# Attention stage of a decoder layer: the last projection unit moved into eight steps of four rows, the newton steps and tile turns of two units respaced

## The chip, the core and the metric

One core of a Trainium2 chip runs the whole kernel. The metric is the device time in microseconds (us); the median of 3 runs of the kernel before is 889.22 us (888.16 to 891.59).

## The reference

```python
def reference(x, p, rel_bias, attn_norm, w_in, ...):
    for i in range(DEPTH):                      # DEPTH = 1, SEQ = 512, D_MODEL = 1024
        h = rms_norm(x, attn_norm[i])
        (mq, mk, mv, nsq, kc, vc, ksl, vsl, kwn, vwn, ngate, mgate) = jnp.split(h @ w_in[i], cuts, axis=-1)
        y_a = moba_attention(rms_norm(mq), rms_norm(mk), mv, tab_moba)          # 8 heads
        y_b = nsa_attention(rms_norm(nsq), kc, vc, ksl, vsl, kwn, vwn, ngate)   # 8 heads, 3 branches
        g_a, g_b = jnp.split(jax.nn.sigmoid(mgate), 2, axis=-1)
        x = x + (g_a * (y_a @ w_br_moba[i]) + g_b * (y_b @ w_br_nsa[i])) @ w_o[i]
        u = causal_dwconv(rms_norm(x, ffn_norm[i]) @ w_up[i], conv_w[i], conv_b[i])
        u_act, u_lin = jnp.split(u, 2, axis=-1)
        x = x + (jax.nn.gelu(u_act) * u_lin) @ w_down[i]
        x = x + jax.nn.sigmoid(x @ w_ple_gate[i]) * (p[i] @ w_ple[i])
    return x
```

The change touches nothing of what is computed. It concerns `h @ w_in`, and the norm over each head of its q and k columns, which are made while the attention of earlier heads runs.

## The kernel before

The kernel is written out by hand for five engines, each with its own instruction stream; semaphores join them. After a start stage comes the attention stage, a list of 100 steps (`STEPS`), and then the dense stages.

**Pairs and steps.** Heads are taken in eight pairs n. Pairs 0 to 3 are MoBA heads and have 8 steps each (two heads e, four query tiles i). Pairs 4 to 7 are NSA heads and have 17 steps each: 8 of the branch slc, 8 of win, and one of cmp. So pair 4 is steps 32 to 48, pair 5 steps 49 to 65, pair 6 steps 66 to 82, pair 7 steps 83 to 99. One step t goes through all engines: `scores(t)` on TensorE (L1629, L1630, or L1625 for cmp), `bias(t)` on VectorE (L1290, or L1298 to L1301 for cmp), `exp(t)` on ScalarE (L886, L883), `invert(t)` on VectorE, which its loop issues one step later behind `bias(t + 1)` (L1308, or L1313 to L1316 for cmp), `scale(t)` on GpSimd (L710, L713), `turn_probs(t)` on TensorE three steps later (L1650, or L1647 for cmp), `take_probs(t)` on ScalarE (L911, L909), and `values` on TensorE five steps later, once for two heads (L1672). `scores(t)` waits for `bias(t - 2)`. Every engine works its steps in order, so an engine that is late with one part of a step is late with all that its stream has behind it.

**Units of the projection.** Beside these steps TensorE works off `h @ w_in` in units w. A unit has 32 rows, one for each of four token tiles tt and eight slices kt of the contraction; a row is three matmuls (`three`, L1491 to L1493), since each float32 operand is held as a high and a low part. Units 5 and 7 have 384 columns, unit 6 has 256. `PROJ` says which rows of which unit stand in which step. Unit 6 serves pairs 5 and 7, unit 7 serves pair 6; the first steps of pair 6 (66 to 69) need unit 7's tiles.

**What a unit needs and sets off.** Its weights come by DMA while the unit before is split. `SPLIT` names the steps in which two slices are split: ScalarE makes both high parts (`w_high`, L843), VectorE the low part of the even slice (`w_low`, L1173), GpSimd that of the odd one (`split_unit`, L683). TensorE waits for both before the row. When a tile's 8 rows are done, ScalarE takes it out of PSUM one step later (`take_proj`, L838), squares it (L853), VectorE sums it (L1224), and for two tiles together makes a first guess of the reciprocal root (`GUESS`, L1148 to L1150). GpSimd refines it in three rounds of four small operations (`ROOT`, L723 to L729), VectorE normalises each tile (`TILE`, L1257), TensorE turns it (`TURN`, L1551), and ScalarE and VectorE store it one step later (L875, L1276). The next tile's turn waits for the one before to be stored, as they share one PSUM bank, and for its own `normalise`.

**Merge gates.** `GATE` places rows of 512 columns of another part of `w_in` (unit j of 8 rows) in the steps; j = 7 has one row in each of steps 41 to 46 and two in 47, j = 8 one in each of 50 to 55 and two in 56. Steps 48, 49 and 57 have none. Their weights are split at `GSPLIT` steps (40 and 48 here): L923 on ScalarE, L1189 on VectorE, L687 on GpSimd.

**Banks.** `proj_bank` puts every tile of units 6 and 7 into PSUM bank 0, so the first row of a tile waits until ScalarE has taken the tile before (`qkv_done`). Bank 7 is that of the gates.

**Order inside a step.** TensorE: scores, `turn_probs(t - 3)`, values, a gate's rows if a tile of the projection opens in this step, the rows of the projection, otherwise the gate's rows here, then the turn of a tile. ScalarE: the gate, `take_proj` and its squares, `take_probs`, the stored tile, `exp`, the gate's split, the weights' split. VectorE: bias, invert, sums, the stored tile, the weights' split, normalise, guess, the gate's split. GpSimd: scale(t - 1), the weights' split, values of the unit, root, the gate's split.

Before the change unit 6 is projected in steps 28 to 35 at four rows a step, its roots stand in steps 33 and 37 (all three rounds in one step), its normalised tiles in 35, 37, 39 and 41, and its turns each one step later. Unit 7 is split in steps 41 to 44, projected in steps 43 to 58 at two rows a step, its roots stand in steps 52 and 60, its tiles in 54, 56, 62 and 64, and its turns one step later.

Of the kernel before, what the change touches and what calls it, by code (L numbers as in the profile page):

```python
# [73 lines left out]
def layer(nc, A, out):  # L74
# [46 lines left out]
    for w in range(2, W_UNITS):  # L121
        b0 = first_t[w - 2]
        if w == 2:
            start, counts, row = b0, (4, 4), ROWS - KT
        elif w < 6:
            start, counts, row = b0 - 4, (5, 6, 5, 5, 6, 5), 0
        elif w == 6:
            start, counts, row = b0 - 4, (4,) * 8, 0
        else:
            start, counts, row = b0 - 6, (2,) * 16, 0  # L130
        for a, count in enumerate(counts):
            PROJ[start + a] = (w, row, row + count)
            row += count
        split0 = b0 - 8 if w == 7 else b0 - 7
        for a in range(KT // 2):
            SPLIT[split0 + a] = (w, range(2 * a, 2 * a + 2))
        VALUES[start + len(counts)] = w
        ends = [t for t in sorted(PROJ) if PROJ[t][0] == w for r in range(*PROJ[t][1:]) if r % KT == KT - 1]
        for half in range(2):
            t = ends[2 * half + 1] + 1 if w > 2 else b0 + 2 * half  # L140
            GUESS[t] = (w, half)
            late = 1 if half and w < 6 else 0
            if late:
                ROOT[t + 1], ROOT[t + 2] = (w, half, range(1)), (w, half, range(1, 3))
            else:
                ROOT[t + 1] = (w, half, range(3))
            if w >= 6:
                late += 1
            for a in range(2):
                TILE[t + 2 + late + 2 * a], TURN[t + 3 + late + 2 * a] = (w, 2 * half + a), (w, 2 * half + a)  # L150

    def segments(t):

# [58 lines left out]
    with ExitStack() as ctx:  # L212
# [186 lines left out]
        def proj_bank(w, tt):  # L399

            if w == 0:
                return (0, 1, 4, 5)[tt]
            if w in (3, 4, 5):
                return 7 * (tt % 2)
            return 6 if w <= 2 and tt % 2 and (w, tt) != (2, 3) else 0

        def column(w, x):
# [1080 lines left out]
        def _(pe):  # L1488
# [22 lines left out]
            def project(w, tt, kts=range(KT)):  # L1511

                c = ucols(w)
                if kts[0] == 0:
                    before = 4 * w + tt - (1 if w > 5 or (w, tt) in ((2, 3), (3, 0)) else 2)
                    if before >= 0:
                        pe.wait_ge(qkv_done, before + 1)
                    if w in (3, 4, 5) and tt == 1:
                        pe.wait_ge(gate_tanh, w)
                for kt in kts:  # L1520
                    wait_weights(pe, w, kt)
                    pe.wait_ge(hT_lo, kt + 1)
                    t_ = slice(P * tt, P * (tt + 1))
                    ins = three(PS[:, proj_bank(w, tt), 0:c], hTh[:, kt, t_], hTl[:, kt, t_], Wh[:, kt, 0:c], Wl[:, kt, 0:c], kt == 0, kt == KT - 1)
                    if tt == NT - 1 and kt < KT - 1:
                        ins.then_inc(w_used, 1)
                if kts[-1] == KT - 1:
                    ins.then_inc(proj_filled, 1)
# [25 lines left out]
            def gate(j, kts=range(KT)):  # L1554

                if kts[0] == 0:
# [4 lines left out]
                        pe.wait_ge(vc_done, 1)  # L1561
                    if j in (3, 4, 5):
                        pe.wait_ge(qkv_done, 4 * j + 4)
                for kt in kts:
                    if kt == 4:
                        pe.wait_ge(g_lo[1], j + 1)
                    ins = three(PS[:, 7, :], Gh[j % 2][:, kt, :], Gl[j % 2][:, kt, :], hTh[:, kt, :], hTl[:, kt, :], kt == 0, kt == KT - 1)
# [360 lines left out]
```

## Time and profile before

| | |
|---|---|
| median of 3 runs | 889.22 us |
| time of the profiled execution | 890.37 us |
| its span, first to last instruction | 888.5 us |
| PE busy | 863.6 us (97%) |
| DVE busy | 378.0 us (43%) |
| ACT busy | 405.8 us (46%) |
| POOL busy | 425.3 us (48%) |

All times below are in us from the start of the span of that one execution. PE is TensorE, DVE VectorE, ACT ScalarE, POOL GpSimd. A row of a timeline gives the start, the duration, the engine, the line of the kernel, the operation and what it writes and reads; behind it, in brackets, how long the engine stood idle before it and who ended the wait. Matmuls are pipelined, so they overlap in the rows, and the distance of two starts is the cost of one. The attention stage runs from about 85 to 364; its steps 32 to 48 from 205.7, steps 49 to 65 from 253.4, step 66 from 294.7.

### The profile page before, as it was taken

To read this page: it belongs to the slowest core of one execution; us is meant where nothing else is said; L and a number is where in the kernel's file an instruction comes from. 1 tells how busy PE (TensorE), PEld (TensorE's weight loads), DVE (VectorE), ACT (ScalarE), POOL (GpSimd) and SP (SyncE) were. 2 spreads that over 40 slices of the span, in tenths; PEclk is the share of its full clock that TensorE was granted. 3 is DMA by queue.
4 is the path that set the end of the run, shared out by engine and by line. 5 is a ranking of instruction groups with operands and counts; after the bars stand their busy time and mean duration, and the time that the engine had idled before them with its cause. 6 is when DMAs were issued, how large, how long until landed. Compare 5 with 4: busy or idle time off the path is not lost.

```text
span 888.5 us, 13023 instructions
## 1 busy us (share of the span) xinstructions
PE 863.6 (97%) x4471; PEld 726.9 (82%) x4471; DVE 378.0 (43%) x864; ACT 405.8 (46%) x882; POOL 425.3 (48%) x547
## 2 busy tenths in 40 slices
PE   8999999999799999999999999999999999999998
PEld 8899889887688776788887888888888888888886
DVE  5446665555545534444417444444444440020223
ACT  5224656566646667533433744444444442231321
POOL 3841764554534345644552644444444444454440
PEclk9999999999999999999999999999999999999999
DMA  6944443342121226266531633333333333332214
GB/s 188 232 109 131 107 103 95 96 113 60 37 60 50 70 85 214 81 233 211 187 95 56 206 94 95 95 98 101 99 97 106 99 98 98 97 102 86 83 62 140
DMA packets 101363, 99.30 MB, mean 112 GB/s; under 512 B 15956, under 2 KB 76084, under 8 KB 101300
## 3 DMA queue, kind: packets, MB, share of 16 engines
q1 hardware_dynamic: 101247, 98.48, 37.7%
q8 instruction: 37, 0.61, 0.3%
q14 instruction: 26, 0.21, 0.1%
q10 hardware_dynamic: 53, 0.01, 0.0%
HBM read 87.58 MB, written 10.88 MB: 111 GB/s over the span
## 4 chain that ended last, share of the span: by engine, by line
PE 88%; DVE 4%; ACT 3%; issue 2%; POOL 2%; SPq 0%; DMA 0%; ACTq 0%; DVEq 0%; POOLq 0%
PE banks L1491 26%; PE banks L1492 25%; PE banks L1493 25%; PE banks L1672 3%; PE banks L1650 2%; PE banks L1630 1%; PE banks L1629 1%; PE banks L1551 1%; PE banks L1680 1%; ACT attention_split L875 1%; DVE plain_arena L1290 1%; DMA plain_arena<-in_conv_w_dram 0%; DVE plain_arena L1257 0%; PE banks L1579 0%; PE banks L1508 0%
## 5 line engine op out<-in xcount | busy, mean ns | idle before, releaser
L698 POOL TENSOR_TENSOR split_arena<-plain_arena,split_arena 128x512 fp32r<-128x512 f32 x184 | 240.2, 1318 | 252.0 <-ACT split_arena L932 232.5
L1491 PE MATMUL banks<-split_arena 128*128 128x512 f32 (+3 forms) x808 | 304.2, 376 | 5.3 <-ACT plain_arena L838 2.1
L1493 PE MATMUL banks<-split_arena 128*128 128x512 f32 (+3 forms) x808 | 296.8, 367 | 0.0
L1492 PE MATMUL banks<-split_arena 128*128 128x512 f32 (+3 forms) x808 | 296.7, 367 | 0.0
L932 ACT ACTIVATE split_arena<-plain_arena 128x512 fp32r<-128x512 f32 x184 | 112.9, 627 | 190.0 <-PE banks L1493 175.2
L1491 PEld LDWEIGHTS banks<-split_arena 128*128 128x128 f32 x808 | 152.4, 189 | 31.9 <-issue 3.5
L1493 PEld LDWEIGHTS banks<-split_arena 128*128 128x128 f32 x808 | 152.0, 188 | 21.1
L1492 PEld LDWEIGHTS banks<-split_arena 128*128 128x128 f32 x808 | 152.4, 189 | 20.3 <-issue 0.5
L1491 PE MATMUL banks<-late_arena,split_arena 128*128 128x512 f32 x240 | 93.8, 391 | 0.0
L1493 PE MATMUL banks<-late_arena,split_arena 128*128 128x512 f32 x240 | 93.5, 390 | 0.0
L1492 PE MATMUL banks<-late_arena,split_arena 128*128 128x512 f32 x240 | 93.5, 389 | 0.0
L1449 DVE SCALAR_TENSOR_TENSOR plain_arena<-banks,plain_arena 128x511 f32<-128x511 f32 x44 | 32.7, 743 | 133.2 <-ACT plain_arena L1041 133.2
L1290 DVE CUSTOM_DVE_ANT_0 plain_arena<-banks,plain_arena 128x128 f32<-128x128 f32 (+1 forms) x96 | 46.8, 487 | 74.0 <-PE banks L1630 73.8
L886 ACT ACTIVATE plain_arena<-plain_arena 128x128 f32<-128x128 f32 (+1 forms) x96 | 53.9, 562 | 37.7 <-DVE plain_arena L1290 37.5
L713 POOL TENSOR_SCALAR plain_arena<-plain_arena 128x128 f32<-128x128 f32 (+1 forms) x64 | 40.0, 627 | 61.3 <-DVE plain_arena L1308 61.1
L911 ACT ACTIVATE attention_plain<-banks 128x128 f32<-128x128 f32 (+1 forms) x96 | 41.3, 430 | 57.9 <-PE banks L1650 57.4
L1493 PEld LDWEIGHTS banks<-late_arena,split_arena 128*128 128x128 f32 x240 | 45.1, 188 | 9.5
L1491 PEld LDWEIGHTS banks<-late_arena,split_arena 128*128 128x128 f32 x240 | 45.1, 188 | 9.2
L1492 PEld LDWEIGHTS banks<-late_arena,split_arena 128*128 128x128 f32 x240 | 45.1, 188 | 9.2
L1650 PE MATMUL banks<-plain_arena 128*128 128x128 f32 x240 | 42.5, 277 | 1.7 <-POOL plain_arena L713 1.7
L1467 DVE TENSOR_TENSOR plain_arena<-banks,plain_arena 128x512 f32<-128x512 f32 x8 | 5.0, 683 | 86.5 <-PE banks L1493 86.5
L1041 ACT ACTIVATE plain_arena<-banks,plain_arena 128x512 f32<-128x512 f32 x44 | 30.6, 777 | 22.3 <-PE banks L1493 22.3
(193 smaller groups left out, 1113.4 us busy)
## 6 DMA issues: line engine op xcount, KB each, us to landing
plain_arena<-in_w_up_dram SPq DMA_DIRECT2D x88, 256.0 KB, 3.2
plain_arena<-in_w_down_dram SPq DMA_DIRECT2D x44, 256.0 KB, 2.6
plain_arena<-in_w_in_dram SPq DMA_DIRECT2D x18, 512.0 KB, 4.2
plain_arena<-in_w_in_dram SPq DMA_DIRECT2D x32, 192.0 KB, 4.0
plain_arena<-in_x_dram SPq DMA_DIRECT2D x8, 512.0 KB, 5.0
gates<-plain_arena SPq DMA_DIRECT2D x16, 256.0 KB, 2.4
plain_arena<-skew SPq DMA_DIRECT2D x16, 256.0 KB, 4.6
plain_arena<-gates SPq DMA_DIRECT2D x16, 256.0 KB, 3.6
```

The costliest lines, as they stand in the source:

```text
L698: pool.tensor_tensor(W2l[:, c % RING, :], raw2[:, c % RING, :], W2h[:, c % RING, :].bitcast(F32), ALU.subtract).then_inc(w2_lo, 1)
L713: pool.tensor_scalar(p_, p_, r, gsig[:, s["i"], h:h + 1], ALU.mult, ALU.mult).then_inc(scaled, 1)
L886: nc.scalar.activation(prob[:, t % 4, 0:nk], prob[:, t % 4, 0:nk], ACT.Exp, bias=mneg[:, t % 4:t % 4 + 1], scale=-1.0, accum_out=rsum[:, t ...
L911: nc.scalar.activation(PT[:, u % 4, 0:i + 1, P * i:P * (i + 1)], PS[:, 4 + t % 2, 0:P * (i + 1)].rearrange("p (j q) -> p j q", j=i + 1), A ...
L932: nc.scalar.activation(W2h[:, c % RING, :], raw2[:, c % RING, :], ACT.Copy).then_inc(w2_hi, 1)
L1041: nc.scalar.activation(dst[:, f % 2, :], PS[:, b, :], ACT.Identity, scale=cst[:, CONVW + 88 + col:CONVW + 89 + col], bias=cst[:, CONVB + c ...
L1290: nc.vector.tensor_tensor_reduce(out=prob[:, t % 4, 0:nk], in0=PS[:, 2 + t % 2, 0:nk], in1=strip[:, n % 2, e, S - nk:S], scale=1.0, scalar ...
L1449: link(nc.vector.scalar_tensor_tensor(out=dst[:, f % 2, 1:S], in0=PS[:, b, 0:S - 1], scalar=cst[:, CONVW + 44 + col:CONVW + 45 + col], in1 ...
L1491: nc.tensor.matmul(o, ah, bh, start=first, stop=False)
L1492: nc.tensor.matmul(o, ah, bl, start=False, stop=False)
L1493: return nc.tensor.matmul(o, al, bh, start=False, stop=last)
L1650: ins = nc.tensor.transpose(PS[:, 4 + t % 2, P * j:P * (j + 1)], prob[:, t % 4, P * j:P * (j + 1)], ident)
```

## The change

Unit 7 is projected at four rows a step in steps 40 to 47 (before: two rows in steps 43 to 58) and its weights are split in steps 38 to 41 (before 41 to 44). So slices 0 to 3 are wanted in step 40, the step after slices 2 and 3 are split, and slices 6 and 7 in step 41, the step in which they are split.

For units 6 and 7 the three rounds of a root stand in three steps in a row, tiles are three steps apart instead of two, and a turn stands two steps behind its tile. Unit 6: roots in 33 to 35 and 37 to 39, tiles in 36, 39, 42, 45, turns in 38, 41, 44, 47. Unit 7: guesses in 44 and 48, roots in 45 to 47 and 49 to 51, tiles in 48, 51, 54, 57, turns in 50, 53, 56, 59, its values taken in 48 (before 59).

Tile 1 of unit 6 goes to bank 7 between two gates, so tiles 1 and 2 of that unit no longer wait for the tile just before; tile 3 still does, and so do all tiles of unit 7.

```diff
         else:
-            start, counts, row = b0 - 6, (2,) * 16, 0
+            start, counts, row = b0 - 9, (4,) * 8, 0
...
-        split0 = b0 - 8 if w == 7 else b0 - 7
+        split0 = b0 - 11 if w == 7 else b0 - 7
...
-            late = 1 if half and w < 6 else 0
-            if late:
+            late = 2 if w >= 6 else half
+            if w >= 6:
+                for r in range(3):
+                    ROOT[t + 1 + r] = (w, half, range(r, r + 1))
+            elif late:
                 ROOT[t + 1], ROOT[t + 2] = (w, half, range(1)), (w, half, range(1, 3))
             else:
                 ROOT[t + 1] = (w, half, range(3))
-            if w >= 6:
-                late += 1
+            gap, lead = (3 if w >= 6 else 2), (2 if w >= 6 else 1)
+            if w >= 6 and half:
+                late += 2
             for a in range(2):
-                TILE[t + 2 + late + 2 * a], TURN[t + 3 + late + 2 * a] = (w, 2 * half + a), (w, 2 * half + a)
+                TILE[t + 2 + late + gap * a], TURN[t + 2 + late + gap * a + lead] = (w, 2 * half + a), (w, 2 * half + a)
...
             if w in (3, 4, 5):
                 return 7 * (tt % 2)
+            if w == 6:
+                return 7 * (tt == 1)
...
-                    before = 4 * w + tt - (1 if w > 5 or (w, tt) in ((2, 3), (3, 0)) else 2)
+                    before = 4 * w + tt - (1 if w > 6 or (w, tt) in ((2, 3), (3, 0), (6, 0), (6, 3)) else 2)
                     if before >= 0:
                         pe.wait_ge(qkv_done, before + 1)
-                    if w in (3, 4, 5) and tt == 1:
+                    if w in (3, 4, 5, 6) and tt == 1:
                         pe.wait_ge(gate_tanh, w)
...
                     if j in (3, 4, 5):
                         pe.wait_ge(qkv_done, 4 * j + 4)
+                    if j == 6:
+                        pe.wait_ge(qkv_done, 4 * 6 + 2)
```

## Rows read from the trace of the kernel before

**Rows 1.** Page, the chain of work that ended last: its shares of the span.

```profile
PE 88%; DVE 4%; ACT 3%; issue 2%; POOL 2%; SPq 0%; DMA 0%; ACTq 0%; DVEq 0%; POOLq 0%
```

**Rows 2.** Waits of PE, 180 to 330: who for whom, total, times, longest.

```profile
PE banks L1551 <- DVE plain_arena L1257: 5.6, 4, 2.6
```

**Rows 3.** Timeline, PE: rows behind its waits for unit 6.

```profile
204.21 0.39 PE L1491 MATMUL banks<-split_arena 128*128 128x256 f32 x1 [1.25 <-ACT plain_arena L838]
...
233.00 0.63 PE L1551 MATMUL banks<-plain_arena 128*128 128x128 f32 x4 [2.58 <-DVE plain_arena L1257]
```

**Rows 4.** Timeline, PE: its three waits in steps 63 to 68.

```profile
288.49 0.66 PE L1650 MATMUL banks<-plain_arena 128*128 128x128 f32 x4 [0.89 <-POOL plain_arena L713]
...
293.95 0.63 PE L1551 MATMUL banks<-plain_arena 128*128 128x128 f32 x4 [0.61 <-DVE plain_arena L1257]
...
299.39 0.66 PE L1647 MATMUL banks<-plain_arena 128*128 128x128 f32 x4 [0.46 <-DVE plain_arena L1316]
```

**Rows 5.** Window: length; PE, PEld, DVE, ACT, POOL busy; PEclk; DMA share, GB/s.

```profile
232.00:238.00 6.00, 5.00 (x22) 4.27 (x24) 4.47 (x14) 4.04 (x12) 2.94 (x5) 0.72 0.29 82
```

**Rows 6.** Timeline, PE: scores of steps 38, 40 and 42; a unit 7 row and what follows.

```profile
220.01 0.33 PE L1629 MATMUL banks<-attention_split 128*128 128x384 f32 x1
...
224.95 0.22 PE L1629 MATMUL banks<-attention_split 128*128 128x128 f32 x1
...
228.77 0.34 PE L1629 MATMUL banks<-attention_split 128*128 128x384 f32 x1
...
245.64 0.34 PE L1491 MATMUL banks<-split_arena 128*128 128x384 f32 x1
...
246.18 0.40 PE L1491 MATMUL banks<-split_arena,attention_split 128*128 128x512 f32 x1
```

**Rows 7.** Timeline, ACT, steps 36 to 41.

```profile
224.41 0.82 ACT L875 ACTIVATE attention_split<-banks,plain_arena 128x256 fp32r<-128x256 f32 x2
225.12 0.72 ACT L886 ACTIVATE plain_arena<-plain_arena 128x512 f32<-128x512 f32 x1
...
227.66 1.04 ACT L923 ACTIVATE split_arena<-plain_arena 128x1024 fp32r<-128x1024 f32 x1
...
230.31 0.92 ACT L843 ACTIVATE split_arena<-plain_arena 128x384 fp32r<-128x384 f32 x2
```

**Rows 8.** Timeline, POOL: first and last of twelve root operations; two splits.

```profile
220.20 0.20 POOL L723 TENSOR_TENSOR plain_arena<-plain_arena 128x8 f32<-128x8 f32 x1
...
223.64 0.20 POOL L729 TENSOR_TENSOR plain_arena<-plain_arena 128x8 f32<-128x8 f32 x1
...
228.78 1.79 POOL L687 TENSOR_TENSOR split_arena<-plain_arena,split_arena 128x512 fp32r<-128x512 f32 x1 [0.62 <-ACT split_arena L923]
...
231.31 0.99 POOL L683 TENSOR_TENSOR split_arena<-plain_arena,split_arena 128x384 fp32r<-128x384 f32 x1 [0.31 <-ACT split_arena L843]
```

**Rows 9.** Timeline, DVE: a stored tile, a normalise, and a slow one.

```profile
220.76 0.89 DVE L1276 SCALAR_TENSOR_TENSOR attention_split<-banks,plain_arena,attention_split 64x256 fp32r<-64x256 f32 x2 [1.07 <-ACT attention_split L875]
221.68 0.69 DVE L1257 TENSOR_TENSOR plain_arena<-plain_arena 128x512 f32<-128x512 f32 x1
...
231.34 1.51 DVE L1257 TENSOR_TENSOR plain_arena<-plain_arena 128x512 f32<-128x512 f32 x1
```

**Rows 10.** Timeline, PE: cmp scores of step 48, their turn in step 51.

```profile
249.90 0.97 PE L1625 MATMUL banks<-attention_split 128*128 128x64 f32 x8
...
256.53 0.66 PE L1647 MATMUL banks<-plain_arena 128*128 128x128 f32 x4
```

**Rows 11.** Timeline, DVE: end of bias(48), gate 9's low part; a tile's sum and guess.

```profile
252.28 0.42 DVE L1301 TENSOR_TENSOR plain_arena<-plain_arena 128x256 f32<-128x256 f32 x1
...
254.14 0.69 DVE L1189 TENSOR_TENSOR attention_split<-plain_arena,attention_split 128x512 fp32r<-128x512 f32 x1 [1.43 <-ACT attention_split L923]
...
258.31 0.42 DVE L1224 TENSOR_REDUCE plain_arena<-plain_arena 128x4 f32<-128x256 f32 x1 [0.66 <-ACT plain_arena L853]
...
259.18 0.17 DVE L1150 TENSOR_SCALAR plain_arena<-plain_arena 128x8 int32<-128x8 int32 x1
```
## The prediction

> **What bounds the kernel now.** I read the views in this order. The page's chain of the work that ended last gives PE 88% of the span [rows 1], so a change in the attention stage is worth what it does to PE's stream and no more: a pause of PE taken away comes off the end, one put in is added. The diff adds and removes no matmul. Then the waits of PE between 180 and 330: the turn of a tile waits for `normalise` four times, 5.6 us in all [rows 2]. PE's own timeline says where: before 233.00 it stood 2.58 us, and before 204.21, at the first row of unit 6's tile 2, 1.25 us for the tile before it in bank 0 [rows 3]. Later, at unit 7, come 0.89 us behind `scale`, 0.61 us for a `normalise` and 0.46 us behind the cmp branch [rows 4]; that 0.61 is the fourth of the four, so unit 6 has 5.6 - 0.6 = 5.0 us. Last the window 232 to 238: a mean granted clock of 0.72 [rows 5], a fall to the lower of the two levels (1.2 for 2.4 GHz) right after the 2.58 us. With PE at work through nearly all of it, that costs (1 - 0.72) x 6 = 1.7 us.
>
> **Part 1, unit 6, a gain.** The bank 0 waits of tiles 1 and 2 go: 1.25 us; tile 3 keeps its wait. The turns move to two steps behind their tiles and the tiles to three apart, so that the store of a tile on ACT and DVE and the next `normalise` (0.89 and 0.69 us on DVE [rows 9]) get over two steps where they had one: 5.0 us go. With them should go the clock fall, as the 2.58 us before it go: 1.7 us. Sum 7.95 us. The roots are the same twelve operations, 220.20 to 223.84, so 0.28 us apart [rows 8], now 1.1 us in each of three steps; unit 7's no longer stand in step 60, where they held `scale` back, so the 0.89 us go as well. The 0.61 us don't pay: what follows, the cmp turn of step 68, comes at the end of a fixed chain from the scores of step 65, and would wait 0.46 + 0.61 instead [rows 4]. Gain in all 8.8 us.
>
> **Part 2, the weights' split, a cost.** PE's 8 rows cost 0.54 us each (two starts 245.64 and 246.18 [rows 6]); that work is only moved. But it wants the weights soon after the split. I take the scores of step 38 as zero (220.01). PE reaches step 40 at 224.95 - 220.01 - 0.87 (the turn's wait there, part of the 5.0) = 4.1 [rows 6]. In steps 38 to 41 ACT now does, one after the other: a strip copy, three pairs of high parts at 0.85 each (0.92 with the end), a stored tile at 0.8, exps of up to 0.7, the gate taken, and gate 8's split at 1.0 [rows 7]. Durations summed, in its order and waiting for bias where it must: slices 0 and 1 are ready at 3.5, 2 and 3 at 6.1, 4 and 5 at 9.5, 6 and 7 at 12.3. On POOL slice 3's low part follows at 7.3 and slice 5's at 10.5 (0.99 each), then in the same step gate 8's low part, 1.79 us, to 12.3, then `scale(40)`, and only then slice 7: 13.7 [rows 8]. PE, with scores and turns between, waits 0.7 and 0.5 us in step 40 (slices 2, 3), and in step 41 1.15, 0.25, 1.4 and 0.75 us (slices 4 to 7). Cost 4.75 us. Queued behind these waits on PE are gate 7's row, the turn of unit 6's tile 1 and all of step 42; nobody but PE loses by it. Check of the sum: step 42 then starts at 15.4, where before it started at 8.76 [rows 6], of which 2.4 were pauses, and eight rows add 4.3: 8.8 - 2.4 + 4.3 + 4.75 = 15.45. Its ends: 1.8 us, if only slices 6 and 7 are late, by a pair's copies and one low part (0.85 + 0.99), and 6 us, if each pair comes 0.4 us later than I sum. I take 4.75, as every term is a row of this stretch.
>
> One term has a port in it. The slow `normalise` (1.51 for 0.69 us [rows 9]) started at 231.34, just behind POOL's low part, 231.31 to 232.30 [rows 8]. The Trainium skill (SBUF — State Buffer, "SBUF: two separate sides") says that a DVE operation with two SBUF inputs and a GpSimd operation that reads SBUF take one port pair as an exclusive lock, and the loser "fully blocks"; by that rule, the trace agrees. By it the `normalise` of step 39, which now meets slice 3's low part, would delay exp(40) and all behind it by up to 0.8 us, and the part would cost 5.5; my sum goes without.
>
> **Part 3, steps 48 to 51, a cost.** Before, six rows of unit 7 (3.2 us) filled the time between the cmp scores of step 48 and their turn in step 51: 256.53 - 249.90 = 6.63 us, nearly without a pause [rows 10]. Now no row is there. PE's own work in this stretch is 6.63 - 3.2 + 0.36 (the turn of unit 7's tile 0) = 3.8 us. And the chain gets longer: after bias(48) (ends 252.70, 2.8 after the scores) DVE now has a sum, a stored tile, a `normalise` and a guess, 0.9 + 0.7 [rows 9] and 0.4 + 0.6 (258.31 to 259.35 [rows 11]), before gate 9's low part and bias(49). Gate 9's low part started 4.24 us after the scores (254.14), waiting for ACT; now DVE gets to it at 2.8 + 2.6 + 0.1 = 5.5, so 1.3 us later [rows 11]. The turn of step 51 comes at 6.6 + 1.4 = 8.0, and PE stands 8.0 - 3.8 = 4.2 us in it, in pieces of at most 1.2 us, since scores(50) waits for bias(48) and scores(51) for bias(49). Bounds: 1.1 us, what PE lost at the next change of pairs (0.61 + 0.46 [rows 4]), and 5 us. I take 4.2. Steps 52 and later have `values` or gates and resemble today's steps 59 to 64; only `scale(57)`, behind gate 10's low part (1.8 us) in a step without a gate row, may be 0.5 us late. I count that.
>
> The other edits cost nothing: PE's wait for the tile before in steps 42, 44 and 46 is covered by a gate row and scores, at least 1.6 us, while ACT is free at the start of those steps; `take_values` in step 48 is one copy on POOL, ahead of gate 9's low part, which waits for ACT anyway; no DMA and nothing of SP's stream moves, as unit 7's weights were loaded in steps 25 to 28; the roots' guess at step 44 has its tile.
>
> **Sum.** -8.8 + 4.75 + 4.2 + 0.5 = +0.6, an exchange of about nine microseconds for nine. On the profiled execution's 890.37 us that is 891.0; the median of the runs is 1.15 lower, so **889.8 us** for the median. A measurement of this kernel can tell about 0.5%, 4.4 us, from no change.
>
> **Rivals.** (a) The splits and the boundary hide better, and the change is faster: both costs at their lower ends, 1.8 + 1.1 + 0 = 2.9, and the full 8.8 gained: 889.2 - 5.9 = 883.3. For it: ACT and POOL have idle time in the trace around these steps, and my chain adds each duration as if nothing slid. Against: the chain is a strict order in the code. 0.2. (b) The clock falls, and the change is slower: PE's rests in step 41 (2.4 us in 3.7) and in steps 50 to 51 (3 us in 3.7) are each as empty as the stretch before 233 that was followed by the half clock [rows 3, 5]. Each fall costs 1.7 us; with two and the port's 0.8: 889.8 + 4.2 = 894.0. It decides from the second fall on. Against: both rests are broken by rows, turns and scores, while the 2.58 us were whole, and in step 41 gate rows follow. 0.14. The Trainium skill (Perfetto Trace Analysis, "Optimization Strategy") says of kernels whose bound changes that "performance may be improved by interleaving those regimes"; the change goes the other way in steps 48 to 58, which is this rival's and part 3's direction. (c) It doesn't do what it says: the turns still wait, because `normalise` slips with DVE's backlog in steps 39 and 42; half of the 5.0 and the clock's 1.7 stay, +4.2: 894.0. Against: PE is itself late there by part 2. 0.06.
>
> **How the numbers follow.** The exchange has 0.6, with its own range 886.5 to 892.5. The 8 in 10 range takes half of (a) and half of (b) and (c): 885.0 to 894.0. Faster than 884.8 is (a) for the most part and a bit of the exchange's low end: 0.2. Slower than 893.7 is (b), (c) and the high end: 0.2. Within: 0.6.
>
> **What would show it.** In the changed kernel's timeline of PE: no wait at the turns (L1551's line) before 240, none at unit 6's tile 2, no clock fall at 233. Waits of the first projection matmul for `w_low` and `split_unit` in steps 40 and 41, 4 to 5 us in sum, the last for POOL. Waits of the scores for bias and of the cmp turn in steps 50 and 51, about 4 us. Fewer than 2 us in either place makes (a); clock windows at half there make (b). Wrong altogether if a wait appears that none of this names, such as a take-over from bank 0 in steps 42 to 46.

## The result, and the profile after

The changed kernel takes 899.19 us (median of 7 runs, 894.03 to 900.81) where the kernel before takes 889.22 (7 runs too, 888.16 to 891.59). It is slower by ten microseconds by the medians. The ratio taken over all runs is 1.0094, with a 95% interval of 1.008 to 1.0108. No difference to be told was forecast (889.8, range 885 to 894).

The profiled execution (899.55 us, span 897.7) has the same matmuls, and PE is busy 4.5 us longer with them (868.1 for 863.6 us): most of that is the lower clock, below. The page's head and its first row:

```profile
span 897.7 us, 13032 instructions
...
PE 868.1 (97%) x4471; PEld 728.9 (81%) x4471; DVE 378.0 (42%) x864; ACT 406.8 (45%) x882; POOL 425.7 (47%) x547
```

The lines of the kernel have moved by 6 to 8: L1551 is now L1557, `normalise` L1263, the projection's first matmul L1497, the low parts L1179 (VectorE) and L689 (GpSimd), the scores L1637. L1296 is bias on VectorE, L1307 the last line of the cmp step's bias, L1322 the end of its invert, L924 the gate taken by ScalarE. The waits of PE from 200 to 310, which answers to [rows 2] (total, times, longest):

```profile
PE banks L1497 <- POOL split_arena L689: 4.2, 3, 1.7
PE banks L1637 <- DVE plain_arena L1296: 3.1, 2, 1.8
PE banks L1557 <- DVE plain_arena L1263: 1.6, 3, 0.7
PE banks L1655 <- DVE plain_arena L1322: 1.3, 2, 0.8
PE banks L1637 <- DVE plain_arena L1307: 1.1, 1, 1.1
PE banks L1497 <- DVE split_arena L1179: 0.8, 1, 0.8
PE banks L1497 <- ACT plain_arena L924: 0.6, 1, 0.6
```

The turn waits of [rows 2] are down from 5.6 to 1.6 us, and the bank wait of [rows 3] is gone. In their place PE waits for the weights' split and, at the change of pairs, for the bias on VectorE. The same stretch of the kernel before has 8.2 us of such pauses, this one 12.9.

The split, on PE's timeline, steps 40 and 41, the rows that wait:

```profile
225.51 0.44 PE L1497 MATMUL banks<-split_arena 128*128 128x384 f32 x1 [0.75 <-DVE split_arena L1179]
...
227.52 0.44 PE L1497 MATMUL banks<-split_arena 128*128 128x384 f32 x1 [1.23 <-POOL split_arena L689]
...
231.08 0.44 PE L1497 MATMUL banks<-split_arena 128*128 128x384 f32 x1 [1.33 <-POOL split_arena L689]
...
234.07 0.69 PE L1497 MATMUL banks<-split_arena 128*128 128x384 f32 x1 [1.67 <-POOL split_arena L689]
```

These are slices 2, 3, 5 and 7; with 0.07 us for slice 4 they make 5.05 us. GpSimd's timeline shows why slice 7 is last: in step 40's part of its stream gate 8's low part (L693) stands between slice 5 and `scale(40)`, and slice 7 comes behind both:

```profile
225.02 1.48 POOL L719 TENSOR_SCALAR plain_arena<-plain_arena 128x384 f32<-128x384 f32 x1
...
228.47 1.59 POOL L719 TENSOR_SCALAR plain_arena<-plain_arena 128x512 f32<-128x512 f32 x1
230.03 0.99 POOL L689 TENSOR_TENSOR split_arena<-plain_arena,split_arena 128x384 fp32r<-128x384 f32 x1
230.98 1.65 POOL L693 TENSOR_TENSOR split_arena<-plain_arena,split_arena 128x512 fp32r<-128x512 f32 x1
232.61 0.45 POOL L719 TENSOR_SCALAR plain_arena<-plain_arena 128x128 f32<-128x128 f32 x1
233.02 0.99 POOL L689 TENSOR_TENSOR split_arena<-plain_arena,split_arena 128x384 fp32r<-128x384 f32 x1
```

The granted clock in two windows (columns as in [rows 5]):

```profile
232.00:241.00 9.00, 7.33 (x27) 6.24 (x26) 1.53 (x6) 2.83 (x7) 2.58 (x4) 0.62 0.23 58
270.00:275.00 5.00, 4.01 (x14) 2.88 (x16) 3.18 (x15) 3.73 (x12) 2.98 (x13) 0.66 0.76 201
```

The engine is at the lower level of its two for (1 - 0.62) x 9 x 2 = 6.8 us from 233 on and for 3.4 us around 271. At half the clock that costs half of these times: 3.4 + 1.7 = 5.1 us, where the kernel before lost 1.7 [rows 5].

Steps 48 to 51 and 57 to 61, the longest waits on PE's timeline:

```profile
266.00 0.39 PE L1637 MATMUL banks<-attention_split 128*128 128x256 f32 x1 [1.12 <-DVE plain_arena L1307]
...
270.47 0.45 PE L1637 MATMUL banks<-attention_split 128*128 128x384 f32 x1 [1.77 <-DVE plain_arena L1296]
...
292.29 0.50 PE L1637 MATMUL banks<-attention_split 128*128 128x512 f32 x1 [1.30 <-DVE plain_arena L1296]
```

**Where the time went.** Pauses: 12.9 - 8.2 = +4.7 us. Clock: 5.1 - 1.7 = +3.4 us. Together 8.1 of the 8.8 us by which step 99 starts later, both counted from the first scores. No run places the other 0.7 us. A listed pause is a little shorter than what is lost (before slice 7 the next matmul would have followed 0.18 us after the one at 232.06 and came 2.01 us after it, where 1.67 are listed), and the changed kernel has six more such pauses; by this estimate they would give about 1 us. Behind the attention stage both kernels run alike.

**The clock differs from run to run.** The mean granted clock of a run tells whether it had falls, but not where. The profiled runs of both kernels have one more fall, in the start stage, which the change doesn't touch; the changed kernel's run in the last experiment doesn't have it. The window 8 to 18 of the changed kernel, and of its run in the last experiment:

```profile
8.00:18.00 10.00, 8.11 (x57) 7.95 (x58) 6.63 (x24) 5.85 (x14) 2.28 (x4) 0.83 0.69 175
8.00:18.00 10.00, 9.18 (x81) 8.73 (x80) 7.86 (x26) 7.35 (x17) 2.45 (x4) 1.00 0.64 174
```

Of the 50 runs of the kernel before that were taken beside the experiments, 18 at a mean clock of 0.999 or 1.000 took 886.4 to 889.1 us (median 887.5), 18 at 0.998 took 888.4 to 890.1, and six at 0.996, the level of the profiled one, took 890.1 to 892.3; the other eight lie at 0.994 to 0.997 with 888.4 to 893.5. The changed kernel took 893.7 to 894.4 in three runs at 0.999, 895.6 in one at 0.995, and 898.9 to 900.8 in eight at 0.991 to 0.993. So without falls the change costs some 6.5 us (894.0 for 887.5), and in its usual runs some 11 (899.8 for the 889.0 of all 50).

### The profile page after: what moved, and what is told of

Read it like the earlier page. It is cut to its first block, busy times and chain, and to the rows that moved or that the text cites. A ratio compares the mean times of both kernels' runs of the same rounds, so it can differ in the third digit from the quotient of the medians.

```text
span 897.7 us, 13032 instructions
## 1 busy us (share of the span) xinstructions
PE 868.1 (97%) x4471; PEld 728.9 (81%) x4471; DVE 378.0 (42%) x864; ACT 406.8 (45%) x882; POOL 425.7 (47%) x547
## 4 chain that ended last, share of the span: by engine, by line
PE 87%; DVE 4%; ACT 3%; POOL 2%; issue 2%; SPq 0%; DMA 0%; ACTq 0%; DVEq 0%; POOLq 0%
PE banks L1497 25%; PE banks L1499 25%; PE banks L1498 25%; PE banks L1680 3%; PE banks L1658 2%; PE banks L1638 1%; PE banks L1637 1%; PE banks L1557 1%; POOL split_arena L689 1%; DVE plain_arena L1296 1%; PE banks L1688 1%; POOL plain_arena L719 1%; DMA plain_arena<-in_conv_w_dram 0%; ACT attention_split L881 0%; ACT split_arena L849 0%
## 5 line engine op out<-in xcount | busy, mean ns | idle before, releaser
L1497 PE MATMUL banks<-split_arena 128*128 128x512 f32 (+3 forms) x808 | 304.5, 377 | 9.0 <-POOL split_arena L689 4.2
L1497 PEld LDWEIGHTS banks<-split_arena 128*128 128x128 f32 x808 | 152.5, 189 | 36.2 <-POOL split_arena L689 5.6
L1497 PE MATMUL banks<-late_arena,split_arena 128*128 128x512 f32 x240 | 93.7, 391 | 0.0
L1296 DVE CUSTOM_DVE_ANT_0 plain_arena<-banks,plain_arena 128x128 f32<-128x128 f32 (+1 forms) x96 | 46.7, 486 | 77.1 <-PE banks L1638 77.1
L1497 PEld LDWEIGHTS banks<-late_arena,split_arena 128*128 128x128 f32 x240 | 45.1, 188 | 9.3
```

Source lines behind the costliest of these rows:

```text
L1296: nc.vector.tensor_tensor_reduce(out=prob[:, t % 4, 0:nk], in0=PS[:, 2 + t % 2, 0:nk], in1=strip[:, n % 2, e, S - nk:S], scale=1.0, scalar ...
L1497: nc.tensor.matmul(o, ah, bh, start=first, stop=False)
```

## The experiments

Eleven kernels, and the changed one once more. All times are medians, beside the kernel before on the same chip (888.4 to 889.3). Where a time is compared with the changed kernel, that is its 899.2 us of above, from another set of runs.

**Unit 6's part alone.** Unit 7's start, split, roots, tiles and turns are put back (excerpt, against the changed kernel):

```diff
-            start, counts, row = b0 - 9, (4,) * 8, 0
+            start, counts, row = b0 - 6, (2,) * 16, 0
-        split0 = b0 - 11 if w == 7 else b0 - 7
+        split0 = b0 - 8 if w == 7 else b0 - 7
```

> The change without its move of unit 7: unit 6's bank 7, its roots in three steps, tiles three apart and turns two behind, while unit 7 is split, projected, rooted and turned as before. Theory A (the waits that the traces show on PE simply add, and a clock fall adds 1.7 us for each 3.4 us at the lower level): the turn waits of 5.0 us, the bank wait of 1.25 us and the fall near 233 go, a turn wait of 0.7 us for unit 5 in step 32 appears, as in the changed kernel; unit 7's three waits (0.89, 0.61, 0.46) stay: 5.0 + 1.25 + 1.7 - 0.7 = 7.3 us faster than before, near 882. Theory B (the respacing itself hurts, because it pushes stored tiles and normalises into step 48 where the cmp chain runs): within 2 us of the kernel before, with new waits in steps 48 to 51.

883.44 us, ratio 0.9929 (0.9909 to 0.9948): the quickest kernel of the study. Its waits from 200 to 310:

```profile
PE banks L1660 <- POOL plain_arena L721: 1.4, 2, 0.9
PE banks L1559 <- DVE plain_arena L1265: 1.3, 2, 0.7
PE banks L1657 <- DVE plain_arena L1324: 0.4, 1, 0.4
PE banks L1639 <- DVE plain_arena L1298: 0.2, 1, 0.2
```

3.4 us for 8.2, and the window 221 to 240 has the full clock (the changed kernel has 0.82 there):

```profile
221.00:240.00 19.00, 18.25 (x109) 14.13 (x108) 11.51 (x38) 15.16 (x44) 13.78 (x23) 1.00 0.15 43
```

Theory A holds, a little short of 7.3 us by the medians (5.5). Part of it is two new waits that it didn't have, 0.25 us for bias (L1639) and 0.49 us behind `scale` (L1660) around step 43; by the profiles the stretch from the first scores to step 99 is 6.4 us shorter. And many runs of before have no fall to lose. Theory B falls.

**Unit 7's part alone.** Unit 6 keeps bank 0, its roots in one step and its spacing (excerpt, against the changed kernel; the lines for bank 7 are taken out as well):

```diff
-            late = 2 if w >= 6 else half
-            if w >= 6:
+            late = 2 if w == 7 else half
+            if w == 7:
...
-            gap, lead = (3 if w >= 6 else 2), (2 if w >= 6 else 1)
+            gap, lead = (3 if w == 7 else 2), (2 if w == 7 else 1)
```

> The other part alone: unit 7 split in steps 38 to 41, projected at four rows in steps 40 to 47, with its new roots, tiles and turns; unit 6 as before (bank 0, roots in one step, tiles two apart, turns one behind). Theory A: waits for the weights' split in steps 40 and 41 of about 5 us, about 4 us in steps 49 to 51, the turn waits of unit 6 (5 us) stay at least by half, and one or two clock falls: 889.2 + 5 + 4 + 1.3 + 1.7 to 3.4 = 901 to 903. Theory B: the move of the rows is harmless: within 2 us of before.

894.57 us, ratio 1.0054 (1.0038 to 1.0071). Some of its waits:

```profile
PE banks L1497 <- DVE split_arena L1179: 2.5, 2, 1.7
PE banks L1653 <- DVE plain_arena L1322: 1.6, 2, 0.8
PE banks L1635 <- DVE plain_arena L1296: 1.6, 2, 1.3
PE banks L1557 <- DVE plain_arena L1263: 1.4, 2, 0.9
```

The direction was right and the size wrong, 894.6 for 901 to 903. The turn waits of unit 6 did not stay by half: only the one in step 38 did (0.87 us). Rows that wait for their weights in steps 40 and 41 (3.3 us) hold PE up, and behind them the tiles are ready. It has one clock fall in the stage (3.4 us long), not more. So the parts don't add up: -5.5 and +5.6 us alone, +10 together. Unit 6's part, which gains 5.5 us alone, costs 4.6 once unit 7's rows stand in steps 40 to 47. The profiles show three causes. It brings PE to step 40 2.4 us earlier, and PE waits longer for the weights (5.05 for 3.3 us). At the change of pairs PE waits 3.86 us, here 2.18: the wait of scores(51) is 1.77 us there and 0.27 here. And the lower clock lasts 10.2 us there and 3.4 here. Of this 1.4 us are won back at the bank and the turns.

The wait of scores(51) shows what Theory B of the first experiment had in mind: with unit 6 respaced, VectorE has one more tile to store in step 48 (0.89 us), and then its first guess (L1154, 0.16 us at 264.47 in unit 7's part alone) takes 1.24 us beside GpSimd's low part of gate 9. The rows are from the changed kernel:

```profile
266.31 0.89 DVE L1282 SCALAR_TENSOR_TENSOR attention_split<-banks,plain_arena,attention_split 64x256 fp32r<-64x256 f32 x2
...
267.84 1.24 DVE L1154 TENSOR_SCALAR plain_arena<-plain_arena 128x8 f32<-128x8 f32 x1
...
267.43 1.62 POOL L693 TENSOR_TENSOR attention_split<-plain_arena,attention_split 128x512 fp32r<-128x512 f32 x1 [2.88 <-ACT attention_split L929]
```

With the rows in place (unit 6's part alone) the same tile in step 48 costs PE nothing.

**Rests filled.** Filler matmuls in step 41, into the free gate bank, ahead of slices 4 to 7:

```diff
                 for kt in kts:
+                    if (w, tt) == (7, 0) and kt >= 4:
+                        if kt == 4:
+                            pe.wait_ge(gate_tanh, 7)
+                        for _ in range((3, 1, 4, 4)[kt - 4]):
+                            nc.tensor.matmul(PS[:, 7, :], hTh[:, 0, 0:P], hTh[:, 1, :], start=True, stop=True)
                     wait_weights(pe, w, kt)
```

> The changed kernel with 12 filler matmuls of 128x512 (3, 1, 4 and 4 ahead of slices 4 to 7 in step 41, into the free gate bank, their result is overwritten) in PE's rests of that step: same waits, busier PE. Theory A, clock part: the fall from 233.3 to 240.1 (6.8 us at the lower level, 3.4 us of time) goes, the waits for the split are not longer by over 0.5 us, so 3 to 3.5 us faster than the changed kernel's 899.2: near 896, or 894 where the second fall is missing too. Rival C (the fall comes of something else than PE's rests in step 41, such as the rests before it): the fall stays and the time is 899 or more.

895.9 us (894.84 to 897.01). The 3.3 us came, but not quite as told: there is no fall from 233 to 240, but one of 3.4 us at 226, right after the 0.75 and 1.22 us rests of step 40, which were not filled. By itself this run decides little, as the changed kernel has a run with just these falls and no fillers (the last experiment: 226 and 267, 895.58 us).

**All rests filled.** The same in steps 40, 41, 50 and 51, 24 fillers (excerpt):

```diff
+                        for _ in range((4, 0, 4, 0, 6)[kt - 3]):
...
+                if t in (50, 51):
+                    pe.wait_ge(qkv_done, 32)
+                    for _ in range(4 if t == 50 else 6):
+                        nc.tensor.matmul(PS[:, 0, :], hTh[:, 0, 0:P], hTh[:, 1, :], start=True, stop=True)
```

> The changed kernel with filler matmuls of 128x512 in PE's rests, 14 in steps 40 and 41 and 10 in steps 50 and 51 (their result is overwritten or not read). Every wait stands as in the changed kernel, within 0.5 us each place; PE is just not idle. Theory A, clock part: no fall of the clock in the attention stage in any run, so all runs lie where the two quick ones of the changed kernel lay, 894.0 to 894.6, none near 899, in spite of 24 more matmuls. Rival C (the clock answers to something else): falls stay and the median is 897 or more.

895.13 us (894.22 to 896.2), none near 899. The clock of its profiled run, from 221 to 240 and from 260 to 275, is 1.00 (the changed kernel has 0.82 and 0.89 there):

```profile
221.00:240.00 19.00, 17.14 (x89) 14.11 (x88) 9.16 (x27) 11.47 (x31) 11.09 (x17) 1.00 0.14 42
260.00:275.00 15.00, 13.41 (x75) 9.02 (x75) 11.47 (x35) 8.75 (x25) 7.79 (x18) 1.00 0.32 89
```

24 matmuls that compute nothing make the kernel 4 us quicker. The falls follow PE's rests: with them filled the profiled run has none, and none of the four runs has a mean clock under 0.997, where eight of the changed kernel's twelve are at 0.991 to 0.993. Two of the four are at 0.997, and their place in the run isn't recorded, so "no fall in any run" is not shown.

**Weights split two steps earlier.**

```diff
-        split0 = b0 - 11 if w == 7 else b0 - 7
+        split0 = b0 - 13 if w == 7 else b0 - 7
```

> The changed kernel with unit 7's weights split two steps earlier (steps 36 to 39, projection still from step 40). Theory A: slices 0 to 5 are ready when PE gets there, slice 7 is no longer behind gate 8's low part on POOL; the waits of the rows in steps 40 and 41 fall from 5.05 us to under 2.5 us and the long clock fall with them: 899.2 - 2.6 - 3.4 = 893. Rival D (ScalarE and GpSimd have more to do in steps 36 to 41 than PE, wherever the split stands): the waits only move, to other lines of steps 38 to 42, and stay at 4 us or more in sum.

893.0 us (889.7 to 896.55). No row waits for its weights any more. Part of it is only moved, to the turns of the probabilities in steps 38 to 42 behind `scale`, 1.6 us of these:

```profile
PE banks L1658 <- POOL plain_arena L719: 1.7, 3, 1.1
```

The median is what theory A said, 6.2 us under the changed kernel, but in part by luck. The profiled run is the quickest of ten (889.7 us): its waits from 200 to 310 are 4.4 us less, not 2.6, and of the falls only one of 3.4 us is left, at 258. The other nine have mean clocks of 0.991 to 0.997, so most of them have more falls; where, isn't recorded. Rival D is right in kind, as some of the wait moved, but not in size.

**Gate 8's split two steps later.**

```diff
-            GSPLIT[t + (3 if t < first_t[4] else 1)] = j + 2
+            GSPLIT[t + (3 if t < first_t[4] or j == 6 else 1)] = j + 2
```

> The changed kernel with the split of gate 8's weights (1.0 us on ScalarE, 0.7 on VectorE, 1.8 on GpSimd) in step 42 instead of 40; they are wanted in step 50. Theory A (slice 7's low part is late as it stands behind gate 8's low part in GpSimd's order): the wait for slice 7 in step 41 (1.67 us) falls below 0.5 us, that for slice 5 (1.33 us) by up to 1 us, and the first clock fall gets shorter or goes: 899.2 - 2.2 - 1.7 to 3.4 = 893.6 to 895.3. Rival G (the high parts on ScalarE set the pace anyway): the wait for slice 7 stays over 1 us, less than 1.5 us gained without the clock.

895.55 us (894.74 to 895.64), just above the 893.6 to 895.3 of theory A. Its waits for slices 5 and 7:

```profile
229.43 0.44 PE L1497 MATMUL banks<-split_arena 128*128 128x384 f32 x1 [1.19 <-POOL split_arena L689]
...
231.14 0.44 PE L1497 MATMUL banks<-split_arena 128*128 128x384 f32 x1 [0.39 <-POOL split_arena L689]
```

Slice 7 waits 0.39 for 1.67 us: it stood behind gate 8's low part. Slice 5's wait hardly changed. The fall at 233 is gone, though PE still rests 0.75, 1.22, 1.19 and 0.39 us within 7 us. The fall at the change of pairs is still there, at 267, and there is one at 287, so 6.8 us at the lower clock for 10.2.

**Rows left for the change of pairs.** Steps 44 to 51 have two rows each:

```diff
-            start, counts, row = b0 - 9, (4,) * 8, 0
+            start, counts, row = b0 - 9, (4, 4, 4, 4, 2, 2, 2, 2, 2, 2, 2, 2), 0
```

> The changed kernel, but only two tiles of unit 7 at four rows a step (steps 40 to 43), the other two at two rows in steps 44 to 51, so that steps 48 to 51 hold eight rows. Theory A: the waits of steps 49 to 51 (3.9 us) fall below 1 us and with them the clock fall at 271; the waits in steps 40 and 41 and the first fall stay: 899.2 - 3 - 1.7 = 894.5. Rival E (the stored tiles, normalise and guess that the respacing puts there hold the chain, rows or not): waits of 2.5 us or more remain in steps 49 to 52 and the time is 897 or more.

891.9 us, 7.3 us under the changed kernel where 4.7 were expected. Of its waits:

```profile
PE banks L1497 <- POOL split_arena L689: 4.2, 3, 1.6
PE banks L1658 <- POOL plain_arena L719: 1.7, 2, 0.9
PE banks L1655 <- DVE plain_arena L1322: 1.4, 2, 0.8
PE banks L1497 <- DVE split_arena L1179: 0.8, 1, 0.8
```

The splits' waits stay as they were, those of steps 49 to 51 fall from 3.9 to 0.7 us (0.10 and one of the two of L1655, 0.61), and the fall at 271 is gone. The first fall is only half as long, 3.4 us, with the same waits ahead of it; why was not tried. The waits of steps 57 to 64 are less too, 1.8 for 2.5 us without the cmp turn, as the last turns moved. That the rows were the cover of the change of pairs is shown. The edit also takes unit 7's second guess out of step 48, but bias(49) still starts 6.6 us after the cmp scores, for 7.1, so that is at most 0.5 of the 3.2 us.

**Gate 10's split two steps later.**

```diff
-            GSPLIT[t + (3 if t < first_t[4] else 1)] = j + 2
+            GSPLIT[t + (3 if t < first_t[4] or j == 8 else 1)] = j + 2
```

> The changed kernel with gate 10's weights split in step 59 instead of 57. Theory A: VectorE's low part of 1.76 us at 290.1 (0.68 elsewhere), with GpSimd's low part beside it, stands before bias(58), for which scores(60) waits 1.30 us; with it out of step 57 that wait falls below 0.4 us, 1 us or so gained: 898 where the clock falls are the same. Rival I (the wait of scores(60) comes from the stored tile and normalise of step 57): it stays at 1 us or more.

895.38 us (893.36 to 897.4). The wait of scores(60) is gone altogether. Here are the three VectorE rows of the changed kernel behind that wait: the stored tile's `normalise`, gate 10's low part, bias(58).

```profile
289.54 0.68 DVE L1263 TENSOR_TENSOR plain_arena<-plain_arena 128x512 f32<-128x512 f32 x1
290.14 1.76 DVE L1195 TENSOR_TENSOR split_arena<-plain_arena,split_arena 128x512 fp32r<-128x512 f32 x1
291.82 0.41 DVE L1296 CUSTOM_DVE_ANT_0 plain_arena<-banks,plain_arena 128x256 f32<-128x256 f32 x1
```

GpSimd's low part of the same gate stands beside the middle one and started first:

```profile
289.89 1.46 POOL L693 TENSOR_TENSOR split_arena<-plain_arena,split_arena 128x512 fp32r<-128x512 f32 x1 [1.98 <-ACT split_arena L929]
```

By the profiles the edit is worth the 1.30 us. The medians differ by more, 3.8 us. The rest isn't the edit's: in its profiled run the waits for slices 5 to 7 are 0.29, 0.86 and 0.50 us, 1.35 us less in sum, with a fall at 227.5 just before them, and it was at the lower level for 6.8 us of the stage, the changed kernel's for 10.2, which is 1.7 us.

**The bank alone.** The kernel before with tile 1 of unit 6 in bank 7 (excerpt; two waits that go with it are left out here):

```diff
+            if w == 6:
+                return 7 * (tt == 1)
...
-                    before = 4 * w + tt - (1 if w > 5 or (w, tt) in ((2, 3), (3, 0)) else 2)
+                    before = 4 * w + tt - (1 if w > 6 or (w, tt) in ((2, 3), (3, 0), (6, 0), (6, 3)) else 2)
```

> The kernel before with one edit: tile 1 of unit 6 in bank 7 and the waits that go with it; no root, tile or turn moves. Theory A: the 1.25 us before tile 2 go, 0.7 us come back at the turn of unit 5's last tile in step 32 and the turn waits of unit 6 may grow as PE comes earlier to them: 0.3 to 1 us faster than before, so between 888 and 888.8, not to be told from it. Rival H (the bank was what made the later turns late): 2 us or more faster, with smaller turn waits.

889.32 us, ratio 0.9998 (0.9983 to 1.0012), not to be told from before, as expected. In the trace the 1.25 us go, 0.72 come back at unit 5's last turn, the three turn waits of unit 6 stand unchanged at 0.87, 1.52 and 2.59. So of the 5.5 us of unit 6's part nearly all is the respacing and the clock.

**Two tries at a better kernel.** Unit 6's part with unit 7 at two rows a step, one step earlier, and its roots in three steps:

```diff
-            start, counts, row = b0 - 9, (4,) * 8, 0
+            start, counts, row = b0 - 7, (2,) * 16, 0
...
-        split0 = b0 - 11 if w == 7 else b0 - 7
+        split0 = b0 - 9 if w == 7 else b0 - 7
...
-            gap, lead = (3 if w >= 6 else 2), (2 if w >= 6 else 1)
+            gap, lead = (3 if w == 6 else 2), (2 if w == 6 else 1)
```

> Unit 6 as in the changed kernel; unit 7 at two rows a step as before but one step earlier (split 40 to 43, rows 42 to 57), its roots in three steps, tiles two apart, turns one behind. Theory A: like the kernel with unit 6's part alone (883.4), without the 0.9 us in which scale stood behind a whole root: 882 to 883, and no clock fall. Rival F: the earlier split meets unit 6's stored tiles and gate 8's split, waits of 1 us and more come up in steps 40 to 44: 884.5 or more.

886.7 us (884.61 to 887.73). Rival F: there are 1.7 us of waits in steps 40 to 44, for low parts and for a scale behind them, and 0.96 at a bank take-over. Unit 6's part with unit 7 where it was, and its roots in three steps (the same, with `b0 - 6` and `b0 - 8`):

> Unit 6 as in the changed kernel, unit 7's split and rows as before (41 to 44, 43 to 58), and unit 7's roots in three steps with its tiles and turns one step later (turns 56, 58, 64, 66; the last is wanted in step 69). Against the kernel with unit 6's part alone (883.4): Theory A says that the 0.9 us in which scale stood behind a whole root go and nothing else moves: 882.5, no wait in steps 60 to 64. Rival F (the later tiles meet the change of pairs at step 65 to 66, stored tile and normalise before the cmp chain's end): the cmp turn of step 68 waits 1 us or more instead of 0.45, and the time is 883.4 or more.

885.25 us (883.6 to 886.66). The 0.9 us behind the root are down to 0.3, but the last turn of unit 7, now in step 66 behind the cmp chain, waits 1.5 us:

```profile
289.52 0.63 PE L1557 MATMUL banks<-plain_arena 128*128 128x128 f32 x4 [1.52 <-DVE plain_arena L1263]
```

Neither beats unit 6's part alone. For the second the ratios to before overlap (0.9923 to 0.9966, and 0.9909 to 0.9948), but the stretch from the first scores to step 99 takes 272.9 us in its profile, where unit 6's part takes 271.8, both without a fall there.

**The changed kernel once more.**

> The changed kernel once more, beside the others on this chip. Theory A: it has two levels with no change in its waits, one near 894 (no fall of the clock in the attention stage, mean granted clock 0.999) and one near 899 (two falls, 10.2 us at the lower level, 0.991), 5.1 us apart; each run lies within 1.5 us of one of them. Rival C: runs spread evenly between them, or the waits differ in the profile.

893.72, 895.58, 900.05, 900.12 and 900.28 us, with mean clocks of 0.999, 0.995, 0.992, 0.992 and 0.991. So the two levels are there, and one run between them that is just outside 1.5 us. Its profile, the 895.58 us run, is of use: the falls are at 226 and 267, 3.4 us each, there is none in the start stage, and the waits for slices 5 to 7 are 0.39, 0.83 and 0.50 us, 1.3 us less in sum than 1.33, 0 and 1.67. The waits do differ then, as rival C had it, and by the clock: PE at half speed comes later to a weight that is ready at the same time (slices 5 and 7 are ready 11.83 and 14.79 us after the scores of step 38, for 11.84 and 14.83). Slice 6 is the exception: its 0.83 us are for VectorE's low part, 1.49 us long here beside GpSimd's, and 0.56 in the first profile. A fall inside a stretch of waits costs less than one that follows it. From the scores of step 38 to those of step 42 this run takes 16.52 us with a whole fall in it. The first profile takes 18.01 with 3.87 us at the lower level, so 16.1 without; by this estimate the fall cost 0.4 us here instead of 1.7.

## Why the prediction was wrong, point by point

**What bounds the kernel** was right: pauses and slow stretches of PE in the attention stage account for 8.1 of the 8.8 us, and nothing behind the stage made up for them.

**Part 1, unit 6.** The turn waits of unit 6 (5.0 us) are gone, and 1.25 us of bank wait, less 0.72 that appeared at unit 5's last turn in step 32, where PE now comes earlier than `normalise`; that rebound wasn't in the sum. The 0.89 us of the root are down to 0.13. Alone the part gave 5.5 us by the medians where it was said to give 7.95 (the root's 0.89 us are not in it). The term that failed in the whole change is the clock's: -1.7 us. The falls went only where the rests went.

**Part 2, the split.** Said 4.75 us, measured 5.05. The chain was right in kind and order, and late by one term: I had slice 3, slice 5 and slice 7 ready 7.3, 10.5 and 13.7 us after the scores of step 38, and they were at 8.3, 11.8 and 14.8 (219.18 is zero; slice 7 ends at 234.01). The difference is for the most part in two scales on GpSimd, of 1.48 and 1.59 us for 0.66 and 0.77, beside VectorE's low parts and `normalise`. VectorE's operations at these two scales (225.02 and 228.47), and two scales of the same sizes with no such operation beside them:

```profile
224.89 0.56 DVE L1179 TENSOR_TENSOR split_arena<-plain_arena,split_arena 128x384 fp32r<-128x384 f32 x1 [0.27 <-ACT split_arena L849]
225.37 0.69 DVE L1263 TENSOR_TENSOR plain_arena<-plain_arena 128x512 f32<-128x512 f32 x1
...
228.31 0.59 DVE L1179 TENSOR_TENSOR split_arena<-plain_arena,split_arena 128x384 fp32r<-128x384 f32 x1 [1.85 <-ACT split_arena L849]
228.82 0.68 DVE L1195 TENSOR_TENSOR split_arena<-plain_arena,split_arena 128x512 fp32r<-128x512 f32 x1
...
285.65 0.66 POOL L719 TENSOR_SCALAR plain_arena<-plain_arena 128x384 f32<-128x384 f32 x1 [0.31 <-DVE plain_arena L1314]
...
287.14 0.77 POOL L719 TENSOR_SCALAR plain_arena<-plain_arena 128x512 f32<-128x512 f32 x1 [0.83 <-DVE plain_arena L1314]
```

That is the port that the prediction held for worth 0.8 us and left out; it was asked of the wrong engine, as GpSimd lost here. The Trainium skill (SBUF — State Buffer, "SBUF: two separate sides") has it that whichever of the two starts first gets the pair for the whole instruction. By that rule, the trace agrees as to who loses, both ways round: 1.51 us on VectorE in [rows 9], 1.48 and 1.59 us on GpSimd here. But each scale sat through a second VectorE operation too, one that started behind it (at 225.37 and 228.82), and ended 0.44 and 0.56 us after that one's end.

**Part 3, the change of pairs.** Said 4.2 us, measured 1.12 + 0.44 + 1.77 + 0.53 = 3.86. The rows were its cover, as the kernel with rows to step 51 shows. That the size came so near is luck: the cmp turn came 8.64 us after the cmp scores and not 8.0, as the guess took 1.24 us beside GpSimd's low part, and PE's own work in the stretch was 4.8 us and not 3.8. The two misses cancel.

**Steps 56 to 68.** I had 0.5 us behind gate 10's split and 1.07 at the cmp turn of step 68, 1.57 in all; measured 0.13 + 0.55 + 0.48 + 1.30 + 0.79 = 3.25. The place was right (gate 10's split in a step without rows), the engine wrong: not `scale(57)` on GpSimd, but bias(58) on VectorE behind a low part of 1.76 us. In this term 1.7 us were missing.

**The clock, the step that failed most.** The prediction's sum takes the fall of before as gone (-1.7 us) and puts the clock of the new rests at nothing, which leaves 0 us at the lower level; measured are 5.1 us of cost. Rival (b) was the mechanism, and it had 0.14. It was under-rated and under-priced in three ways. I took the fall of the kernel before as a sure gain of 1.7 us, from one profiled run; it is there in some runs only. I priced a fall at 1.7 us, but the first one lasted 6.8 us and cost 3.4. And I argued that rests broken by rows and turns would not do what a whole rest of 2.58 us did; they did: the longest single rest of the changed kernel is 1.77 us. 5.1 for 0 us is the largest part of the miss, 1.7 in steps 56 to 68 the next, then 0.7 in step 32 and 0.3 in the split, less 0.3 at the change of pairs. That sums to 7.5 on a forecast of +0.6, so 8.1, and the rest are the 0.7 us that no run places. The clock isn't all of it: in the three runs without falls the change still costs some 6.5 us, where the forecast without its clock term is +2.3. The range left out what it should have held: the sum of two terms in doubt and the clock at once.

Rivals (a) and (c) fell: the costs stood at their middle, and no turn of unit 6 waits.

## What to carry to other kernels

Work that an engine is bound by is also the cover of everything beside it. When it is moved, price the place it leaves (here 3.9 us at the change of pairs, 1.3 us at a gate's split) like the place it goes to (5.05 us, for weights wanted in the step in which they are split). And price a set of rests for what it does to TensorE's clock as well, which here came to as much as the rests themselves; a change that thins out PE's work has this on top, and one profiled run doesn't say how often. Try the parts of a change apart: here one was worth -5.5 us and the other +5.6, and together they made +10, since the first brings PE earlier to the second's waits and puts one more tile to store into step 48, where the second leaves no rows.

## What the runs showed of the hardware

- TensorE's clock fell after rests of at most 1.8 us with work between them, not only after a whole one. In the changed kernel's profile it stood at the lower level for 6.8 and 3.4 us; eight of its twelve runs have as low a mean clock (0.991 to 0.993), and three have 0.999. With 24 filler matmuls in the rests the profile has neither fall, and the kernel takes 4 us less. Rests like these don't bring a fall in every run: with gate 8's split later the profile has none after 0.75, 1.22, 1.19 and 0.39 us.
- Of two waits on the same weight, the one with the lower clock just before it was shorter (0.39 for 1.33 us), and the weight was ready at the same time (11.83 and 11.84 us after the scores of step 38): rests and falls don't simply add.
- GpSimd's scale took 1.48 and 1.59 us for 0.66 and 0.77 beside two-input operations of VectorE, and VectorE's low part 1.76 for 0.68 beside GpSimd's (290.14 and 289.89). A guess of eight elements took 1.24 for 0.16 us beside it (267.84 and 267.43).
